# Sink heads with stationary values in two column groups, and a later wait for reread constants

## The reference

```python
def sink_softmax(scores, sink):
    full = jnp.concatenate([scores, jnp.broadcast_to(sink, scores.shape[:-1] + (1,))], axis=-1)
    return jax.nn.softmax(full, axis=-1)[..., :-1]
...
    p = sink_softmax(jnp.concatenate([s_ctx, s_loc], axis=-1), sk)
    p_ctx = p[..., :C].astype(v.dtype)
    p_loc = p[..., C:].astype(v.dtype)
    o = jnp.einsum('bngrqk,bkgd->bnqgrd', p_ctx, vc) + jnp.einsum('bngrqk,bnkgd->bnqgrd', p_loc, vband)
...
    y = of * lax.rsqrt(jnp.mean(of * of, axis=-1, keepdims=True) + EPS) * g.astype(jnp.float32)
...
        x = x + mod[:, 2, None] * (jnp.concatenate([o_a, o_b, o_c], axis=-1) @ w_out[l])
```

## Time and profile before

| | us |
|---|---|
| median of 3 runs | 1123.78 |
| lowest and highest | 1120.91, 1124.18 |
| the profiled execution | 1134.15 |
| its span | 1132.3 |
| TensorE busy | 942.2 (83%) |
| VectorE busy | 453.1 (40%) |
| ScalarE busy | 248.3 (22%) |
| GpSimd busy | 195.4 (17%) |

### The profile page before, as it was taken

How to read it: one execution, slowest core, us unless ns; L and a number is a source line. 1 busy time by engine, 2 the same in 40 slices (tenths; PEclk the granted TensorE clock), 3 DMA queues, 4 the chain that set the end, 5 groups by cost and what they waited for, 6 DMA issues and landing times.

```text
span 1132.3 us, 23611 instructions
## 1 busy us (share of the span) xinstructions
PE 942.2 (83%) x9000; PEld 566.8 (50%) x9000; DVE 453.1 (40%) x1074; ACT 248.3 (22%) x491; POOL 195.4 (17%) x327
## 2 busy tenths in 40 slices
PE   3999999988898399989878389999998378876795
PEld 2536446555455256868544166543654144443453
DVE  2177425655554323323222386416732412221133
ACT  2100112443322023223222031123521012111121
POOL 4100000110010134444424220001100111110011
PEclk9999999999989599999999789999998589897898
DMA  9997602830003999999999968317504989999992
GB/s 347 383 403 294 258 25 75 326 111 1 1 1 127 393 372 409 417 420 413 412 408 413 391 264 311 137 45 268 230 1 146 399 356 416 416 413 401 416 398 91
DMA packets 53901, 314.49 MB, mean 278 GB/s; under 512 B 6780, under 2 KB 7616, under 8 KB 34864
## 3 DMA queue, kind: packets, MB, share of 16 engines
q1 hardware_dynamic: 42752, 286.93, 63.1%
q0 software_dynamic: 8432, 17.92, 4.5%
q10 hardware_dynamic: 2624, 8.27, 1.9%
HBM read 307.24 MB, written 9.50 MB: 280 GB/s over the span
## 4 chain that ended last, share of the span: by engine, by line
PE 63%; DMA 22%; issue 7%; DVE 5%; DVEq 2%; ACT 1%; SPq 1%; POOLq 0%; POOL 0%; ACTq 0%
PE ps L1941 59%; DMA ring<-in_w 11%; DMA area<-in_w 5%; DMA ring<-in_w_in 2%; DMA HT<-in_w 2%; PE ps L2222 2%; DMA area<-h_rows,area 1%; DMA cst<-in_w 1%; PE ps L2051 1%; PE ps L2072 1%; DMA expert_rows<-area 1%; DVE area L1609 1%; PE ps L2252 0%; PE ps L2241 0%; DVE area L1444 0%
## 5 line engine op out<-in xcount | busy, mean ns | idle before, releaser
L1941 PE MATMUL ps<-ring,area 128*32 128x256 f32 x3520 | 217.3, 402 | 60.9 <-issue 30.1
L1941 PE MATMUL ps<-ring,HT 128*128 128x512 f32 (+1 forms) x576 | 258.6, 602 | 2.0 <-ACT HT L1164 1.4
L1941 PEld LDWEIGHTS ps<-ring,area 128*32 128x32 f32 x3520 | 135.9, 115 | 138.3 <-issue 66.5
L1941 PE MATMUL ps<-area 128*32 128x256 f32 (+4 forms) x1976 | 183.3, 391 | 25.9 <-DVE area L1828 9.7
L1941 PEld LDWEIGHTS ps<-ring,HT 128*128 128x128 f32 x576 | 110.4, 197 | 128.1 <-issue 126.0
L1941 PEld LDWEIGHTS ps<-area 128*32 128x32 f32 (+3 forms) x1976 | 118.2, 150 | 67.4 <-issue 43.1
L1856 DVE STREAM_TRANSPOSE area<-area 128x256 f32<-128x256 f32 x65 | 29.0, 446 | 188.3 <-PE ps L1941 188.0
L949 POOL DMA_INDIRECT area<-h_rows,area x68 | 71.1, 1046 | 110.3 <-DVEq L1841 42.4
L1941 PE MATMUL ps<-HT,ring 128*128 128x256 f32 (+1 forms) x320 | 87.1, 430 | 2.7 <-DMA ring<-in_w_in 2.6
L1941 PEld LDWEIGHTS ps<-HT,ring 128*128 128x128 f32 x320 | 60.9, 193 | 23.6 <-issue 14.4
L1444 DVE SCALAR_TENSOR_TENSOR area<-area,CW 128x512 f32<-128x512 f32 (+1 forms) x120 | 68.8, 614 | 4.5 <-issue 0.5
(11 more groups left out here) (231 smaller groups left out, 862.0 us busy)
## 6 DMA issues: line engine op xcount, KB each, us to landing
ring<-in_w SPq DMA_DIRECT2D x56, 2048.0 KB, 10.7
ring<-in_w_ada SPq DMA_DIRECT2D x24, 2048.0 KB, 15.1
ring<-in_w_in SPq DMA_DIRECT2D x10, 2048.0 KB, 15.2
area<-in_w SPq DMA_DIRECT2D x20, 1024.0 KB, 10.9
HT<-in_w SPq DMA_DIRECT2D x8, 2048.0 KB
area<-in_w SPq DMA_DIRECT2D x8, 2048.0 KB, 11.2
late<-in_w SPq DMA_DIRECT2D x8, 1536.0 KB
ring<-in_w_out SPq DMA_DIRECT2D x4, 2048.0 KB, 8.7
```

The source lines that it names most:

```text
L1941: return t_.matmul(out, lhsT, rhs, start=first, stop=last_)
```

## The change

In five parts:

- A sink pair has one O instead of two. The values of the key head, 128x64, are the stationary operand, and the transposed probabilities of head a stream past it into partitions 64a to 64a + 63 of bank 6. The result is already transposed, and VectorE copies it straight into `HT`. Bank MB, its transposes and ScalarE's copy are gone.
- Since the result can no longer be scaled by a column for each query, `probs` multiplies the probabilities of both heads by their reciprocal sums before T.
- The squares for the head norm follow block 3, and M of a tile comes right behind the O of its last pair; the last M stands before that O. The filler of the next tile therefore starts earlier, and in layer 0 all but two steps of it are used inside the list.
- `out_part` takes the blocks in the order 0, 1, 2, 3, 6, 7, 4, 5 and waits for the sink blocks alone at the last two. ScalarE's `second` for the first tiles moves behind the list.
- The wait for the reread constants moves to `channel_sums("mu")`, for both layers.

```diff
+OUT_ORDER = (0, 1, 2, 3, 6, 7, 4, 5)
+
+
+def out_job(l, x):
+
+    n, m = t_jobs(l)[x]
+    return x if m or units_of(l)[n][1] < BLK_A else x + 1
+
...
         out += [("T", x) for x, (a, _) in enumerate(tj) if a == n]
-        out += [("O", x) for x, (a, _) in enumerate(tj) if a == n - 1]
+        out += [("O", x) for x, (a, _) in enumerate(tj) if a == n - 1 and out_job(l, x) == x]
         if l == 0 and n == 5:
             out.append(("C",))
         if l and n == 4:
             out.append(("F",))
         if l and n == 6:
             out.append(("B",))
-        if units[n][1] == 2 and units[n][0] > 0:
+        if units[n][1] == 0 and units[n][0] > 0:
             out.append(("M", units[n][0] - 1))
             heads_out.add(units[n][0] - 1)
-    out += [("O", x) for x, (a, _) in enumerate(tj) if a == len(units) - 1]
+    out.append(("M", nq - 1))
+    out += [("O", x) for x, (a, _) in enumerate(tj) if a == len(units) - 1 and out_job(l, x) == x]
     while dense:
         fill(KD)
-    out.append(("M", nq - 1))
...
-                        wait_made(act, ("O", l, k - 2))
+                        wait_made(act, ("O", l, out_job(l, k - 2)))
...
+                for i in range(nq - 2):
+                    second(i)
...
                     else:
                         v.tensor_tensor(sums[:, b], sums[:, b], es[:, b], ALU.add)
                         dve.drain()
-                        v.reciprocal(rec[:, n % 4], sums[:, b]).then_inc(pr_done[l], 1)
+                        v.reciprocal(rec[:, n % 4], sums[:, b])
+                        dve.drain()
+                        for m in range(2):
+                            last = v.tensor_scalar(PB[:, b, m, 0:kw], PB[:, b, m, 0:kw], rec[:, n % 4, m:m + 1], None, ALU.mult)
+                        last.then_inc(pr_done[l], 1)
 
                 def take_o(k):
                     n, m = tj[k]
                     i, u = units[n]
                     key = ("O", l, k)
                     wait_made(dve, key)
+                    if u >= BLK_A:
+                        taken(v.tensor_copy(HT[:, u, i * P:(i + 1) * P], bank(key)[:, 0:P]), key)
+                        return
                     if u == 0 and i >= 2:
-                        wait_made(dve, ("MB", l, i - 2))
-                    w = P if u < BLK_A else HD
-                    taken(v.tensor_scalar(O[i % 2][:, u * P + m * HD:u * P + m * HD + w], bank(key)[:, 0:w], rec[:, n % 4, m:m + 1], None, ALU.mult), key)
-                    if u == BLK - 1 and m == 1:
+                        wait_made(dve, ("MA", l, i - 2))
+                    taken(v.tensor_scalar(O[i % 2][:, u * P:(u + 1) * P], bank(key)[:, 0:P], rec[:, n % 4, 0:1], None, ALU.mult), key)
+                    if u == BLK_A - 1:
 
...
-                take_dense(ended)
+                if ended:
+                    take_dense(ended)
...
                 if l == LATE[0]:
                     for k in range(KD - 4):
                         ada_part(*LATE, k)
-                    pe.wait_ge(cst2_in, 32)
...
                     if name == "mu":
+                        pe.wait_ge(cst2_in, 16 * (l + 1))
                         pe.wait_ge(cv_d, l + 1)
...
                         wait_taken(pe, ("MA", l, i))
-                        wait_taken(pe, ("MB", l, i))
-                    last = mm(bank(key), HT[:, k, i * P:(i + 1) * P], ring[:, slot(l, ("out", h)), k], k == 0, k == KD - 1)
+                    block_ = OUT_ORDER[k]
+                    if BLK_A <= block_ < BLK:
+                        x_, = [x for x, job in enumerate(tj) if job == (i * BLK + block_, 1)]
+                        wait_taken(pe, ("O", l, x_))
+                    last = mm(bank(key), HT[:, block_, i * P:(i + 1) * P], ring[:, slot(l, ("out", h)), block_], k == 0, k == KD - 1)
                     if k == KD - 1:
                         made(last, key)
...
                         key = ("O", l, x_)
+                        if u >= BLK_A:
+                            wait_taken(pe, ("T", l, x_ - 1))
                         wait_taken(pe, ("T", l, x_))
                         claim(pe, key)
-                        c0, w = (u * P, P) if u < BLK_A else (512 + (u - BLK_A) * HD, HD)
                         nkt = 4 if i < 2 else 2
                         for kt in range(nkt):
-                            last = mm(bank(key)[:, 0:w], aT[:, x_ % 2, kt * P:(kt + 1) * P], V[:, 4 - nkt + kt, c0:c0 + w], kt == 0, kt == nkt - 1)
+                            ks = slice(kt * P, (kt + 1) * P)
+                            if u < BLK_A:
+                                last = mm(bank(key)[:, 0:P], aT[:, x_ % 2, ks], V[:, 4 - nkt + kt, u * P:(u + 1) * P], kt == 0, kt == nkt - 1)
+                                continue
+                            c0 = 512 + (u - BLK_A) * HD
+                            for a in range(2):
+                                last = mm(bank(key)[HD * a:HD * (a + 1), 0:P], V[:, 4 - nkt + kt, c0:c0 + HD], aT[:, (x_ - 1 + a) % 2, ks], kt == 0, kt == nkt - 1)
                         made(last, key)
...
+                        key = ("MA", l, x_)
+                        claim(pe, key)
+                        for b in range(BLK_A):
+                            last = t_.transpose(bank(key)[:, b * P:(b + 1) * P], O[x_ % 2][:, b * P:(b + 1) * P], ident)
+                        made(last, key)
```

12 lines of the change are left out of this document (removed).

## The result

| | before | after |
|---|---|---|
| median of 20 runs each, us | 1127.06 | 1120.76 |
| ratio, 95% interval | | 0.9939, 0.9921 to 0.9957 |
| the profiled execution | 1134.15 | 1123.23 |
| its span | 1132.3 | 1121.3 |

The change makes the kernel faster by 0.61%, about 6.9 us by the ratio. The forecast was 2.2 us, "within 0.3%" (3.4 us), so the gain came out at twice that band. The time of 1120.76 lies beside the predicted 1121.5 by chance: the base of 1123.78 came from 3 runs, and 20 put it at 1127.06; the base was 3.3 us too low and the gain over 4 us too small, and the two nearly cancel.

The account below looks back on a forecast made before the run. TensorE was taken to bound both attentions, the only part edited. Layer 0 gained 2.8 us and layer 1 lost 0.6; with no clock difference, 1123.78 less 2.2 gave 1121.6, rounded to 1121.5 us; range 1112 to 1129.

Parts of the forecast that it names:

- Sum: Both attentions at full clock: layer 0 gains 2.8 us, layer 1 loses 0.6, together 2.2 us gained.
- Sink products: A sink pair over 512 keys: 2.38 us becomes 1.04, from expert rows with column groups; the Trainium skill's packing rule gave 3.2.
- Multiplications: Scaling a sink pair's probabilities on VectorE before the transposes: 0.8 us for both, 0.5 over 256 keys.
- Squares ahead of pair 5: Squares before pair 5's probabilities, 1.5 us; its transposes 3.2 us later in tile 0, 3.4 wait in layer 1 tile 1.
- Head norm: TensorE's wait before head-norm transposes: four in layer 0, 6.65 us with ScalarE's store; two in layer 1, 1.4 and 1.35.
- Bank 7, mod columns, head 0 of tile 1: Layer 0 waits: two output products for a bank held by residual addition 0.4, 1.15 us; mod columns 0.95; head 0 1.1.
- The logits: End of layer 0's attention: TensorE waits 3.6 us before the first logits, behind VectorE's addition, ScalarE's squares and columns.
- Added waits of layer 0 together: All new waits in layer 0's attention at full clock: 17.9 us added against 20.7 gone, a gain of 2.8.
- Constants: Head of layer 1: moving the wait for the reread constants to the channel sums is worth nothing.
- The clock: Clock falls behind waits of 2 us or longer: 7.4 us layer 0, 3.9 layer 1; 11.3 against 11.2, no difference.
- The clock stays up: Rival: in the attentions only waits of 3 us and more bring a clock fall; 10.0 us gained, 1114 us; chance 0.36.
- The others: Rivals: constants held TensorE, 1110 us, chance 0.02; clock falls slow it, 1130.5, 0.13; column groups not overlapping, 1128.5 or 1143.5, 0.07.

Follow-up runs that it names:

- e4_serial: The changed kernel with the eight products of a sink pair ordered by head instead of alternating: 1124.07 us, ratio to before 0.9963.
- e6_second: The changed kernel with ScalarE's squares of tile 2 in layer 0 moved behind its first columns: 1117.32 us, ratio to before 0.9916.
- e1_const: The kernel before with only the wait for the reread constants moved to the channel sums: 1128.10 us, ratio to before 1.0007.
- e3_cols: The changed kernel with the old places of M, head squares, filler and ScalarE's first-tile squares, keeping the column groups: 1110.10 us, ratio to before 0.9836.

## Why the forecast was right or wrong, by its own steps

**Sum.** Two profiles of each kernel give, for both attentions: at full clock 230.1 before and 225.5 after, so 4.6 us won where the prediction had 2.2; lost by the clock 16.2 before and 13.6 after, so 2.6 us won where it had -0.1. Together 7.2, beside 6.9 measured. The sum agrees; the division between the two is uncertain by some 2 us by these profiles, and the last column of the table has more of it on the clock.

**Sink products.** 1.09 us (0.66 over 256 keys) against 1.04: right, and the argument from the expert rows held against the rule. That a long pair needs the alternating order for it and a short one doesn't (e4_serial) was not seen.

**Multiplications.** Both together take 0.88 us against 0.8. Right.

**Squares ahead of pair 5.** With the multiplications, 0.65 + 2.20 in tile 0 of layer 0 against 3.25, and 0.65 + 3.17 in tile 0 of layer 1 against 3.2; in tile 1 of layer 1 3.25 against 3.4. Right in the main, 0.6 us too small in tile 0 of layer 1.

**Head norm.** 1.0, 1.3, 1.8, 1.0 and 0.5 for the store, 5.6 us, against 6.65; 1.9 against 2.75 in layer 1. Too large by a quarter: where no residual addition is in front, copy and norm (0.29 and 0.68 us) and both hand-overs pass in 0.99 us, and I had 0.3 us more for the hand-overs.

**Bank 7, mod columns, head 0 of tile 1.** 0.3 and 0.9, 0.85, 0.87 against 0.4 and 1.15, 0.95, 1.1: right.

**The logits.** 2.69 against 3.6. The chain is the right one (e6_second), 0.9 us too long by my count from ends to starts.

**Added waits of layer 0 together** come to 14.5 us, not 17.9. But layer 0 gained 3.8 us at full clock and not 6.2, so what I let go (20.7) was also too much, by 2.4 us. The two profiles of before differ by as much in this layer (143.7 and 141.6 at full clock), so no term need be wrong for it.

**Constants.** Nothing: right (e1_const).

**The clock: the step that failed.** "At 1.7 us for each such place and a longer one in the crowded tile 0 I get 7.4 us for layer 0 and 3.9 for layer 1, 11.3 against 11.2." In layer 0 the places were right and the charge wasn't: a wait of about 2 us is not a fall for certain. Layer 0 lost 3.4 and 6.8 us in two profiles of the changed kernel, 8.5 and 10.3 in two of the one before: 4.3 us won, not 0.7. In layer 1 the forecast looked at too few places. It counted two falls before, 3.1 us, and left out a third under the last output product; two stretches of the profile before (columns as in the earlier trace rows):

```profile
859.00:864.00 5.00, 4.22 (x21) 3.29 (x19) 0.40 (x1) 0.91 (x2) 0.00 (x0) 0.71 0.98 334
864.00:869.00 5.00, 5.00 (x8) 2.01 (x7) 0.00 (x0) 0.00 (x0) 0.00 (x0) 0.61 0.43 170
```

So layer 1 lost 6.8 us before and not 3.1, and 8.5 after and not 3.9; such a fall came under the last output product in both profiles of the changed kernel too. It grew by 1.7 us, in the direction forecast, and with 0.9 us won at full clock layer 1 lost 0.8 us in all, against 1.4. I had also read the clock of before from a single profile. That the granted clock over both attentions would move by at most 0.03 held: from 0.94 to 0.95 in the first profile of each, since layer 0 rose (0.95 to 0.98) and layer 1 fell (0.95 to 0.92).

**The rivals.** "The clock stays up" had 10.0 us; the 6.9 measured lie between it and the forecast, where the prediction had said that half cases lie. Of its condition one half came: layer 0 kept the clock better, layer 1 didn't. The others didn't come.

**What the prediction didn't see.** It costed each part and never asked what the change would be without one of them. For layer 0 its own terms would have given the sign: the order adds 6.65 (norm), 1.55 (bank 7), 3.6 (logits) and 1.5 (squares), 13.3 us, and removes 5.1, 3.2 and 0.5, 8.8 us, a loss of 4.5. Profiles of the changed kernel and of e3_cols show 3.0 us at full clock and 1.7 by the clock there, and 1.3 and 3.4 in layer 1, 9.4 beside the 10.7 between the medians. The column groups alone were worth 17.0.

## What to carry to other kernels

When a change has two parts, sum each alone: here a saving of 17.0 us was handed in with a reordering that took 10.7 of it back. Work moved forward on an engine that a second engine waits for is paid at the next hand-over; move it behind the last thing that is waited for, and look at the first and last tile apart, where nothing covers a wait. And don't price a fall of the clock at its full size behind a wait of about 2 us: take two or more profiles of before, read them to the very end of the stage, and count such falls as possible, not as certain.
